# A second buffer of probabilities, score banks released after the mask, and one modulation chunk beside each pair of heads in the last mixers

## The reference, cut to what matters

```python
mx = jnp.split((jax.nn.silu(c) @ w_mod[l] + b_mod[l])[:, None, :], N_MOD, axis=-1)
x = x + 0.5 * mx[2] * swiglu(modulate(rms_norm(x), mx[0], mx[1]), ...)       # ffn1
hx = modulate(rms_norm(x), mx[3], mx[4]) @ w_in[l]
hz = modulate(rms_norm(z), mz[3], mz[4]) @ w_in[l]
mix_x, mix_z = token_mixing(hx, hz, ...)
x = x + mx[5] * (mix_x @ w_out[l])
x = x + 0.5 * mx[8] * swiglu(modulate(rms_norm(x), mx[6], mx[7]), ...)       # ffn2
# inside token_mixing, four heads each, head width 64:
s = concat([q @ k_window * scale + bias, q @ k_ctx * scale]); p = softmax(s)   # neighbourhood heads
s = q @ concat(k_x, k_z) * scale;                             p = softmax(s)   # grouped heads
o = p @ concat(v_x, v_z)
```

## Time and profile before

| | us |
|---|---|
| median of 3 runs | 3158.82 (3157.44 to 3159.85) |
| the profiled execution, its own time | 3160.95 |
| span of its trace | 3159.1 |
| PE busy | 3022.9 (96% of the span) |
| DVE busy | 1800.9 (57%) |
| ACT busy | 1482.2 (47%) |
| POOL busy | 151.6 (5%) |

### The profile page before, as it was taken

How to read it: one execution, slowest core, us unless ns; L and a number is a source line. 1 busy time by engine, 2 the same in 40 slices (tenths; PEclk the granted TensorE clock), 3 DMA queues, 4 the chain that set the end, 5 groups by cost and what they waited for, 6 DMA issues and landing times.

```text
span 3159.1 us, 54007 instructions
## 1 busy us (share of the span) xinstructions
PE 3022.9 (96%) x23072; PEld 2759.9 (87%) x23072; DVE 1800.9 (57%) x2813; ACT 1482.2 (47%) x2222; POOL 151.6 (5%) x147
## 2 busy tenths in 40 slices
PE   7999999999999999999999889999999999999998
PEld 5899888898889997899898679999899999989997
DVE  4455555655556445454645454465756656586665
ACT  3345445453555443345444334456654445665443
POOL 0000000001000000000200000001010101111000
PEclk9999999999999999999999989999999999999999
DMA  7765445654555556754365155554355654435563
GB/s 273 280 217 164 159 150 188 210 200 138 165 188 173 178 197 218 253 202 162 120 188 165 67 189 198 187 175 134 102 168 190 201 187 157 128 112 163 166 200 133
DMA packets 409691, 556.65 MB, mean 176 GB/s; under 512 B 25277, under 2 KB 357997, under 8 KB 409069
## 3 DMA queue, kind: packets, MB, share of 16 engines
q1 hardware_dynamic: 409452, 553.20, 52.6%
HBM read 552.12 MB, written 1.05 MB: 175 GB/s over the span
## 4 chain that ended last, share of the span: by engine, by line
PE 83%; DVE 8%; DMA 3%; ACT 3%; issue 2%; SPq 0%; POOL 0%; DVEq 0%; ACTq 0%
PE psum L119 24%; PE psum L121 23%; PE psum L120 23%; PE psum L710 1%; DMA wr<-in_ffn_w_dram 1%; PE psum L1893 1%; DVE wl L276 1%; DVE wl L2151 1%; PE psum L2316 1%; PE psum L1183 1%; PE psum L2422 1%; PE psum L2400 1%; PE psum L1528 1%; PE psum L1878 1%; DMA wr<-in_w_out_dram 1%
## 5 line engine op out<-in xcount | busy, mean ns | idle before, releaser
L276 DVE TENSOR_TENSOR wl<-wr,wh 128x1024 fp32r<-128x1024 f32 (+1 forms) x558 | 658.0, 1215 | 237.0 <-ACT wh L265 236.2
L265 ACT ACTIVATE wh<-wr 128x1024 fp32r<-128x1024 f32 (+1 forms) x558 | 555.0, 1040 | 262.1 <-DMA wr<-in_ffn_w_dram 228.5
L119 PE MATMUL psum<-xt_hi,wh 128*128 128x256 f32 (+1 forms) x2000 | 565.9, 283 | 4.0 <-DVE wl L276 3.0
L120 PE MATMUL psum<-xt_lo,wh 128*128 128x256 f32 (+1 forms) x2000 | 558.1, 279 | 0.0
L121 PE MATMUL psum<-xt_hi,wl 128*128 128x256 f32 (+1 forms) x2000 | 557.9, 279 | 0.0
L2151 DVE TENSOR_TENSOR wl<-wr,wh 128x1024 fp32r<-128x1024 f32 (+3 forms) x336 | 391.9, 1201 | 123.0 <-ACT wh L2143 121.7
L119 PEld LDWEIGHTS psum<-xt_hi,wh 128*128 128x128 f32 (+1 forms) x2000 | 377.3, 189 | 16.1 <-issue 8.7
L120 PEld LDWEIGHTS psum<-xt_lo,wh 128*128 128x128 f32 (+1 forms) x2000 | 376.9, 188 | 2.3
L121 PEld LDWEIGHTS psum<-xt_hi,wl 128*128 128x128 f32 (+1 forms) x2000 | 377.8, 189 | 0.1
L119 PE MATMUL psum<-wh,xt_hi 128*128 128x256 f32 (+1 forms) x1280 | 371.2, 290 | 6.6 <-DVE wl L276 4.8
L2143 ACT ACTIVATE wh<-wr 128x1024 fp32r<-128x1024 f32 (+3 forms) x336 | 322.7, 998 | 103.8 <-DMA wr<-in_mlp_w_dram 74.4
(11 more groups left out here) (466 smaller groups left out, 5396.4 us busy)
## 6 DMA issues: line engine op xcount, KB each, us to landing
wr<-in_ffn_w_dram SPq DMA_DIRECT2D x231, 1024.0 KB, 5.2
wr<-in_w_in_dram SPq DMA_DIRECT2D x88, 1024.0 KB, 5.1
wr<-in_w_mod_dram SPq DMA_DIRECT2D x72, 1024.0 KB, 4.9
wr<-in_mlp_w_dram SPq DMA_DIRECT2D x64, 1024.0 KB, 5.2
wr<-in_w_out_dram SPq DMA_DIRECT2D x20, 1024.0 KB, 5.9
wr<-in_mem_w_kv_dram SPq DMA_DIRECT2D x8, 1024.0 KB, 4.9
wr<-in_w_branch_dram SPq DMA_DIRECT2D x16, 512.0 KB, 3.5
wr<-in_w_branch_dram SPq DMA_DIRECT2D x8, 1024.0 KB, 5.0
```

Of the source, the lines that this page charges most:

```text
L119: pe.matmul(out, a[0], b[0], start=first, stop=False)
L120: pe.matmul(out, a[0], b[1], start=False, stop=False)
L265: act.activation(self.high[s][:, r], self.raw[s][:, r], ACT.Copy).then_inc(self.highs.sem, 1)
L276: dve.tensor_tensor(self.low[s][:, r], self.raw[s][:, r], self.high[s][:, r].bitcast(F32), ALU.subtract).then_inc(self.lows.sem, 1)
```

## The change: what it does, and the diff

1. In the last mixers (`l == 1`) the buffer of probabilities holds two pairs, `[P, 4, 512]`, in another place of SBUF; pair i uses half `i % 2`. `exp` of pair i waits for the transposes of pair i-2 instead of i-1. (In layer 0 `deep` is 1 and the wait is what it was.)
2. `score` of pair i+1 waits for `emptied` of pair i: for a pair with a bias that is the second masking instruction (L1919) of DVE, for one without the second exponential, as before. The masking instruction now counts on a semaphore of its own, `masked`; DVE's own wait behind it stays.
3. `M1[26]` keeps 6 steps; `M1[27]` to `M1[33]` have 1 step each in place of 6.

```diff
+        self.masked_n = [sum("bias" in un for pair in pairs[:i] for un in pair) for i in range(n + 1)]
+        self.masked = w.share("head_masked", self.masked_n[n])
+        self.deep = buf["p"].shape[1] // 2
...
+    def probs_of(self, i, t):
+        return self.buf["p"][:, 2 * (i % self.deep) + t, :]
+
+    def emptied(self, pe, i):
+
+        if self.masked_n[i + 1] > self.masked_n[i]:
+            pe.wait_ge(self.masked.sem, self.masked.at(self.masked_n[i + 1]))
+        else:
+            pe.wait_ge(self.probs.sem, self.probs.at(2 * i + 2))
...
-        if i >= 1:
-            act.wait_ge(self.turned.sem, self.turned.at(2 * i - 1 + t))
+        if i >= self.deep:
+            act.wait_ge(self.turned.sem, self.turned.at(2 * (i - self.deep) + t + 1))
...
-            link(dve.scalar_tensor_tensor(out=two(buf["sm"][:, t, 0:m]), in0=two(src), scalar=HD ** -0.5, in1=un["bias"], op0=ALU.mult, op1=ALU.add))
+            dve.scalar_tensor_tensor(out=two(buf["sm"][:, t, 0:m]), in0=two(src), scalar=HD ** -0.5, in1=un["bias"], op0=ALU.mult,
+                                     op1=ALU.add).then_inc(self.masked.sem, 1)
+            dve.wait_ge(self.masked.sem, self.masked.at(self.masked_n[i] + t + 1))
...
                 if i >= 1:
-                    pe.wait_ge(self.probs.sem, self.probs.at(2 * i))
+                    self.emptied(pe, i - 1)
                 self.score(pe, i, 0)
...
-            self.buf = dict(att, p=own(s, l, "probs", [P, 2, 512], 0))
+            self.buf = dict(att, p=own(s, l, "probs", [P, 2, 512], 0) if l == 0 else own(Z, l, "probs", [P, 4, 512], 8))
...
-    for p_ in M1[26:34]:
-        p_.steps = 6
+    M1[26].steps = 6
+    for p_ in M1[27:34]:
+        p_.steps = 1
```

More of the change, by code:

```diff
@@ L1884, in turn @@
             for j in range(self.width(i) // P):
-                last = pe.transpose(self.w.ps[:, bank + t, j * P:(j + 1) * P], self.buf["p"][:, t, j * P:(j + 1) * P], self.w.eye)
+                last = pe.transpose(self.w.ps[:, bank + t, j * P:(j + 1) * P], self.probs_of(i, t)[:, j * P:(j + 1) * P], self.w.eye)
             last.then_inc(self.turned.sem, 1)
@@ L1899, in exp @@
         act.wait_ge(self.peaks.sem, self.peaks.at(2 * i + t + 1))
-        if i >= 1:
-            act.wait_ge(self.turned.sem, self.turned.at(2 * i - 1 + t))
+        if i >= self.deep:
+            act.wait_ge(self.turned.sem, self.turned.at(2 * (i - self.deep) + t + 1))
         src = buf["sm"][:, t, 0:m] if masked else self.w.ps[:, bank + t, 0:m]
-        act.activation(buf["p"][:, t, 0:m], src, ACT.Exp, bias=buf["neg"][:, t, 0:1], scale=1.0 if masked else HD ** -0.5,
+        act.activation(self.probs_of(i, t)[:, 0:m], src, ACT.Exp, bias=buf["neg"][:, t, 0:1], scale=1.0 if masked else HD ** -0.5,
                        accum_out=buf["sums"][:, 2 * (i % 2) + t, 0:1]).then_inc(self.probs.sem, 1)
```

## The result

| | before | after |
|---|---|---|
| median, us | 3159.05 (4 runs) | 3134.90 (4 runs, 3131.32 to 3138.58) |
| profiled execution, us | 3160.95 | 3135.46 |
| span, us | 3159.1 | 3133.7 |

The direction and the main mechanism hold; the size does not.

What follows compares the result with a forecast made beforehand. Bound: TensorE, 96% busy, with the projection 12.4 us late for a `w_out` chunk whose slot was blocked. `x_out1` starting at 1824.6 instead of 1840.57 gains 16.0 us: 3158.82 - 16.0 = 3142.8, predicted 3143, range 3138 to 3150.

Steps and rivals of the forecast that it cites:

- The hole in the transfers: Transfers at 1760 to 1865 us: one chunk in 52 us, making the output projection 12.4 us late.
- The step with a chunk: Attention steps: each takes 5.29 us with a modulation chunk beside it, bounds 4.3 and 6.8.
- The placing of steps by pieces: Attention steps 0 to 6 come with `M1[27]` to `M1[33]`; steps 7 to 9 and MixTurn's four with `x_out1`.
- the transfers under cover: Chunk loads hide behind attention steps; uncovered, each chunk would show as about 2.9 us.
- DVE's added 0.63: A chunk's transpose and addition add 0.63 us per attention step on DVE, hidden by 0.6 us.
- Rivals A to C: A: chunks only move, 3153.5, chance 0.10; B: `w_out` split exposed, 3148, 0.10; C: half clock holds on, 3177, 0.03.
- C: Attention steps 0 to 6: half clock holds on, steps about 10.2 us instead of 5.29, up to 3177; chance 0.03.
- The start. ... I keep the half clock to 1781.4.: First attention steps: half clock kept to 1781.4, score 3 at 1787.7; up to 2 us less if it returns sooner.
- Its first 3.4 us ran at clock 0.50 ... so I leave it.: Start of `x_out1`: half clock there cost 1.7 us, assumed to stay and kept as a bonus in the range.
- Score 3 to the first transpose of `mix`: Later attention: score 3 at 1787.7, steps of 5.29 us, first transpose of `mix` at 1819.8 instead of 1823.43.
- The `w_out` split: Late attention: splitting `w_out` chunks on ACT and DVE exposes 0.4 us before score 7 and delays ACT 0.8.
- both clock terms: Full clock at the attention's start (2.0 us) and from `x_out1`'s first product (1.7): 3139, in the range only.

Runs made afterwards that it cites:

- before, again: The kernel before, no edit, traced a second time: 3163.48 us in a single execution, 97.92 us from first score to squares.
- the second pair: Second traces of the kernels before and after, neither edited: 97.92 and 73.75 us from first score to squares.
- one buffer: The kernel after with one buffer of probabilities again (edits 2 and 3 only): 3137.64 us, ratio to before 0.9939.
- the two filled variants of before: The kernel before with added identity products, either in front of attention steps without a chunk or before `x_out1`: 3153.48 and 3154.39 us, ratios 0.9993 and 0.9987.
- before, x_out1 filled: The kernel before with 14 identity products instead of 4 in front of the first piece of `x_out1`: 3154.39 us, ratio 0.9987.
- steps only: The kernel before with edit 3 alone (`M1[27]` to `M1[33]` at 1 step each): 3142.43 us, ratio to before 0.9945.
- late banks, start filled: The kernel after without edit 2, with 12 and 5 identity products before scores 1 and 2: ratios to before 0.9925 and, again, 0.9932.

## Why the prediction was wrong

**Right.** The hole in the transfers and what it costs: MixTurn to `x_out1` was forecast at 4.8 us and took 4.82. The step with a chunk, read from one single pair of scores of before: 5.29, measured 5.28 to 5.29 four times. The placing of steps by pieces, the transfers under cover, DVE's added 0.63 hidden. Rivals A to C did not come: scores are 5.29 apart, none waits over 1 us, the clock did not stay low. (C's price was near: a step at half clock was put at 4.9 us more, and in before, again, one took 9.91, 4.6 more.)

**Wrong: the clock, left as it was.** In the cut stretch the sum said 16.0 us; the traces say 94.70 - 73.40 = 21.3, and 24.2 between the second pair. The 5.3 us between are, term by term (rounded); the first two are the steps of the prediction that failed:

- *"The start. ... I keep the half clock to 1781.4."* First score to score 3 was put at 15.9 us (1771.8 to 1787.7) and took 13.57: 2.3 us, net of the 1.0 by which step 2 to 3 took longer than its 5.3. The half clock was not a given of the place but went with the idle time ahead of score 1. Score 1 took 2.08 us in all six traces of kernels that lack the chunks or the early release and aren't filled, both of before among them; it took 1.35 in one and 1.13 in the other seven. Of the traces of kernels whose first scores wait for exponentials and aren't filled, five of five show a granted clock of 0.74 to 0.96 from 1770 to 1810 (partly filled: 0.91); of the seven that have chunks and either the early release or a filled start, five show 1.00 and two 0.96.
- *"Its first 3.4 us ran at clock 0.50 ... so I leave it."* `x_out1` to the squares was left at 25.96 and took 23.57: 2.4 us, of which 1.5 is the clock. From its first product to the first result on DVE (L1256) the five traces with the wait for `w_out` show 7.2 to 8.4 us, the nine without it 5.7 to 5.9. So the lower clock goes with the wait; what of the wait brings it is not shown, as said above. The other 0.8 is no clock but the wider spacing of products in the last section: "one buffer" has it without the lower clock and took 24.41, the second trace of before lacks it and took 25.05.
- Score 3 to the first transpose of `mix`: 32.1 forecast, 31.44 measured, 0.7. The `w_out` split was to show 0.4 before score 7 and did not, because with edit 1 ACT gets to it earlier; "one buffer" shows what it would have been, 1.24.

A third low stretch was in the 16.0 without being named. In before, score 7 to the first transpose of `mix` took 13.74 us, and 13.78 the second time, with the transposes of pair 7 at half clock (1.92 us at 1817.63); in the two filled variants of before they took 1.04, and this part 12.15. The forecast went through it at full-clock durations, so 1.6 of its 16.0 us were clock already. The first line is of before, the second of "before, x_out1 filled":

```profile
1817.63 1.92 PE L1885 MATMUL psum<-eye,probs 128*128 128x128 f32 x8
```

```profile
1816.68 1.04 PE L1885 MATMUL psum<-eye,probs 128*128 128x128 f32 x8
```

I had both clock terms as a bonus of 3.7 us in the range and left them out of the forecast. The trace of before had the sign in it: the clock's low stretches in the earlier trace rows each stand beside idle time that the change removes. The Trainium skill says in TensorE: Matmul & The Clock Gate (What's actually happening) that the slow level is the default and activity lifts it. The traces here agree with the direction of it, not with certainty for the length: the same code had its low stretch to 1782.6 us once and to 1793 once, and after had none once and one of 3.4 us once.

**And the range.** The rest, from 21.3 to the 24.1 or 23.8 us of the medians, is not resolved by place, and its cause stays open: the profiled pair has 4.2 us outside the stretch, 1.3 ahead of it and 2.9 behind, and the two traces of after differ there by 5.4 and 3.0 us. An estimate from the spacing of the products in the two traces: 0.9 of the 1.3 and 1.4 of the 2.9 are the wider spacing of the last section, which fell more often on before. Before's own later medians (3156.31 to 3159.49) move the gain by as much. A part can be that a profiled execution of before is one draw: the second had 97.92 in the stretch. The range's lower end stood 5 us under the forecast, 3.7 of them for the two clock terms, which left 1.3 for all that differs from one execution to the next.

**A reason given wrongly.** The prediction had edits 1 and 2 as what "must let the next score start" at 5.29. The pair of scores that gave 5.29 ran with the old waits, and "steps only" shows the old waits harmless there. Their worth is at the two ends of the attention, 5.5 us in the trace (1.1 of it the lower clock), 8.0 in the medians.

## What to carry to other kernels

A ring of transfers stops when the consumer's program puts long work between two small users of it; the bill comes at the first large user behind. Look for the hole in the DMA rate, and spread the small users over the long work, where they also fill its waits. And when a change fills idle time of TensorE, price the lower clock that stands beside that idle time as likely gained, not as a bonus; read more than one trace of the same kernel, since one trace shows one draw.

## What the runs showed of the hardware that was not expected

At a granted clock of 1.00 products of one shape (128x256) come at two spacings. The 48 products of a `w_out` piece take 5.44 us in ten of the fourteen traces and 5.65 in four, nothing between, and the two traces of one kernel ("late banks, start filled") have one each. Before's first trace is among the four; that is the 0.8 us of its 25.96. It is not a property of an execution: every trace has both. In after, the products from 1754.79 to 1759.03 stand 0.118 us apart and those from 1820.71 to 1830.23 stand 0.113 apart. Over 1100 to 1200 us the mean spacing is 0.113 in all fourteen traces, over 2500 to 2600 it is 0.118 in all fourteen; at other places, as at `x_out1`, it differs from trace to trace. The granted clock doesn't show it (1.00 in both), and the runs don't show what sets it. DVE's timeline in before and in after:

```profile
1848.05 0.69 DVE L1256 TENSOR_TENSOR gated_rows<-psum,gate_rows 128x512 f32<-128x512 f32 x1 [4.52 <-PE psum L121]
1853.70 0.69 DVE L1256 TENSOR_TENSOR gated_rows<-psum,gate_rows 128x512 f32<-128x512 f32 x1 [1.84 <-PE psum L121]
```

```profile
1831.57 0.69 DVE L1256 TENSOR_TENSOR gated_rows<-psum,gate_rows 128x512 f32<-128x512 f32 x1 [1.63 <-PE psum L121]
1837.01 0.69 DVE L1256 TENSOR_TENSOR gated_rows<-psum,gate_rows 128x512 f32<-128x512 f32 x1 [1.63 <-PE psum L121]
```
